# Two recurrent layers on one core: 32x32 inverses turned by VectorE, delta scores paired, single steps moved by one half slot

## What is computed

```
dq, dk_, dv_ = split(causal_conv_silu(dn_qkv)); dq, dk_ = l2norm(dq), l2norm(dk_)
# per head: with the decay between tokens and beta, strictly lower A = beta * (k k^T) * decay
# T = (I + A)^-1 ; u = T (beta v) ; o = (q k^T * decay) u
h_b = rmsnorm(o, dn_norm_w) * silu(dn_z)
```

```
h_a = rmsnorm(mlstm(q, k, v, i, f)) * ml_norm_w * sigmoid(ml_o) * silu(ml_z)
y = sigmoid(gate_a) * (h_a @ w_out[:2048]) + sigmoid(gate_b) * (h_b @ w_out[2048:])
```

## Time and profile before

| what | value |
|---|---|
| median of 3 runs | 2379.36 us (2378.09 to 2380.82) |
| profiled execution, own time | 2380.18 us |
| its span, first to last instruction | 2378.4 us |
| PE busy | 2362.0 us (99%) |
| DVE busy, ACT busy, POOL busy | 1426.4, 1183.9, 241.7 us |

### The profile page before, as it was taken

How to read it: one execution, slowest core, us unless ns; L and a number is a source line. 1 busy time by engine, 2 the same in 40 slices (tenths; PEclk the granted TensorE clock), 3 DMA queues, 4 the chain that set the end, 5 groups by cost and what they waited for, 6 DMA issues and landing times.

```text
span 2378.4 us, 28485 instructions
## 1 busy us (share of the span) xinstructions
PE 2362.0 (99%) x11452; PEld 1939.2 (82%) x11452; DVE 1426.4 (60%) x1701; ACT 1183.9 (50%) x1695; POOL 241.7 (10%) x336
## 2 busy tenths in 40 slices
PE   9999999999999999999999999999999999999998
PEld 7887888888888888888887778788888888888887
DVE  6655665665566545665865565576554554557775
ACT  6544454454445444555655455465444444446554
POOL 0053004305300430000000010000000000000000
PEclk9999999999999999999999999999999999999999
DMA  6565457446545655666665454456555555655554
GB/s 211 195 173 164 142 178 190 157 154 183 167 137 182 174 169 169 222 206 194 211 216 190 142 179 149 152 179 227 186 188 195 189 184 194 193 181 193 195 194 142
DMA packets 241073, 430.79 MB, mean 181 GB/s; under 512 B 32212, under 2 KB 35933, under 8 KB 240942
## 3 DMA queue, kind: packets, MB, share of 16 engines
q1 hardware_dynamic: 227808, 413.38, 54.4%
q10 hardware_dynamic: 13134, 15.60, 2.2%
HBM read 423.66 MB, written 5.29 MB: 180 GB/s over the span
## 4 chain that ended last, share of the span: by engine, by line
PE 89%; POOL 5%; DVE 2%; DMA 1%; issue 1%; ACT 1%; ACTq 0%; SPq 0%; POOLq 0%; DVEq 0%
PE gemm L1328 27%; PE gemm L1330 27%; PE gemm L1329 27%; POOL arena L2283 5%; PE side L904 3%; DMA arena<-delta_blocks 1%; DVE arena L1751 1%; DVE weight_lo L1745 1%; PE side L1251 1%; PE side L998 0%; PE side L1266 0%; PE side L1290 0%; DMA arena<-in_x_dram 0%; PE side L1064 0%; PE side L1220 0%
## 5 line engine op out<-in xcount | busy, mean ns | idle before, releaser
L1745 DVE TENSOR_TENSOR weight_lo<-weight_raw,weight_hi 128x1024 fp32r<-128x1024 f32 x780 | 970.5, 1248 | 736.3 <-ACT weight_hi L1356 735.0
L1356 ACT ACTIVATE weight_hi<-weight_raw 128x1024 fp32r<-128x1024 f32 x780 | 821.9, 1056 | 863.2 <-PE gemm L1330 822.7
L1328 PE MATMUL gemm<-weight_hi,x_hi 128*128 128x512 f32 x2368 | 943.8, 399 | 1.1 <-DVE weight_lo L1745 1.1
L1330 PE MATMUL gemm<-weight_hi,x_lo 128*128 128x512 f32 x2368 | 924.6, 390 | 0.0
L1329 PE MATMUL gemm<-weight_lo,x_hi 128*128 128x512 f32 x2368 | 924.0, 390 | 0.0
L1328 PEld LDWEIGHTS gemm<-weight_hi,x_hi 128*128 128x128 f32 x2368 | 445.4, 188 | 100.2 <-issue 9.7
L1330 PEld LDWEIGHTS gemm<-weight_hi,x_lo 128*128 128x128 f32 x2368 | 445.2, 188 | 94.3
L1329 PEld LDWEIGHTS gemm<-weight_lo,x_hi 128*128 128x128 f32 x2368 | 445.9, 188 | 88.9 <-issue 1.4
L1328 PE MATMUL gemm<-weight_hi,lhs_hi 128*128 128x512 f32 x736 | 287.4, 390 | 0.0
L1330 PE MATMUL gemm<-weight_hi,lhs_lo 128*128 128x512 f32 x736 | 286.8, 390 | 0.0
L1329 PE MATMUL gemm<-weight_lo,lhs_hi 128*128 128x512 f32 x736 | 286.7, 390 | 0.0
(11 more groups left out here) (186 smaller groups left out, 1024.0 us busy)
## 6 DMA issues: line engine op xcount, KB each, us to landing
weight_raw<-in_w_in_dram SPq DMA_DIRECT2D x207, 1024.0 KB, 5.1
weight_raw<-in_w_out_dram SPq DMA_DIRECT2D x48, 1024.0 KB, 5.1
weight_raw<-in_w_gate_dram SPq DMA_DIRECT2D x44, 1024.0 KB, 5.2
weight_raw<-in_w_up_dram SPq DMA_DIRECT2D x44, 1024.0 KB, 5.1
weight_raw<-in_w_down_dram SPq DMA_DIRECT2D x44, 1024.0 KB, 5.0
arena<-rel_line ACTq DMA_DIRECT2D x8, 384.0 KB, 5.3
arena<-delta_blocks ACTq DMA_DIRECT2D x16, 128.0 KB, 5.2
arena<-in_x_dram ACTq DMA_DIRECT2D x4, 512.0 KB, 6.0
```

The lines of the kernel that those rows point to most:

```text
L1328: e.matmul(pair[i][:, :], xh[:, s], wh, start=first, stop=False)
L1330: m = e.matmul(pair[i][:, :], xl[:, s], wh, start=False, stop=last)
L1356: return e.activation(o, i, ACT.Copy, scale=scale)
L1745: return e.tensor_tensor(o, x, y, op)
```

## The change

1. `dT` moves from PE and ACT to DVE: one `transpose` instruction on the whole tile of 128x1024 (eight 128x128 matrices), which turns each 32x32 block in place of its own. It waits for `tin`. The two PSUM banks of `dT` and its two ACT copies are gone.
2. The tile `N` of `dinv` now counts as live until `tout` has landed, so its block is given out later, and the homes of many later tiles differ.
3. The six `dsc` steps stand two a half slot: s+8 to s+10 in place of s+8 to s+13.
4. `dnorm` (all four groups, q and k), the chain `mnum`, `msq`, `mgated`, `mout` of pr = 1 and 3, and `gout` of the second pair of GLA heads stand one half slot later.

```
-            put(END[key] + 7, "dnorm", key, 0), put(END[key] + 7, "dnorm", key, 1)
+            put(END[key] + 8, "dnorm", key, 0), put(END[key] + 8, "dnorm", key, 1)
...
-            put(s + 8 + z, "dsc", g, q)
+            put(s + 8 + z // 2, "dsc", g, q)
...
-        put(s + 31, "dT", g, 0), put(s + 31, "dT", g, 1)
+        put(s + 31, "dT", g)
...
-        s = END[f"mz{pr}"] + 2 if pr % 2 else END[f"dz{pr}"] + 45
+        s = END[f"mz{pr}"] + 3 if pr % 2 else END[f"dz{pr}"] + 45
...
-    put(t + 1 + hp, "ggated", hp), put(t + 2 + hp, "gout", hp, 0), put(t + 2 + hp, "gout", hp, 2)
+    put(t + 1 + hp, "ggated", hp), put(t + 2 + 2 * hp, "gout", hp, 0), put(t + 2 + 2 * hp, "gout", hp, 2)
...
-        live(("N", g), ("nin", g), ("pool:dinv", g))
+        live(("N", g), ("nin", g), ("dma:tout", g))
...
-        live(("U", g), ("dT", g, 0), ("pe:du1", g))
+        live(("U", g), ("dT", g), ("pe:du1", g))
...
-        def dT(g, i):
-            w.wait_ge(*at("dma:tin", g))
-            p, Tt = open_bank("dT", g, i), heads(blk("Tt", g), i)
-            for h in range(HB):
-                m = turn(p[:, h * P:(h + 1) * P], Tt[:, h, :])
-            m.then_inc(sem("pe:dT"))
...
-        def dT(g, i):
-            U = claim("U", g)
-            w.wait_ge(*at("pe:dT", g, i))
-            copy(part(U, i), bank("dT", g, i)).then_inc(sem("act:dT"))
...
+        def dT(g):
+            U = claim("U", g)
+            w.wait_ge(*at("dma:tin", g))
+            e.transpose(U, blk("Tt", g)).then_inc(sem("dve:dT"))
```

More of the change, by code:

```diff
@@ L398 @@
 for _engine, _names in {
-        "pe": "cols0 cols xturn gate1 fsum rel1 convturn dnorm dsc dT dX dv du0 dbu du1 do dout chan mdec mscore "
+        "pe": "cols0 cols xturn gate1 fsum rel1 convturn dnorm dsc dX dv du0 dbu du1 do dout chan mdec mscore "
               "mturn mnum mout ggate2 gsum gscore gkend gstate go gout alog aturn apv fturn",
-        "act": "xturn sqsum kept tanh convtap convsilu dnorm dT du0 du1 donorm dout chan mexp mturn msq mout "
+        "act": "xturn sqsum kept tanh convtap convsilu dnorm du0 du1 donorm dout chan mexp mturn msq mout "
                "ggabs ggexp ggln gkend gsq gout aexp aturn apv fturn",
-        "dve": "cols xturn kept silu gate0 gate2 fsum rel0 rel1 convtap convsilu ddecay dsc dX dv dbu do "
+        "dve": "cols xturn kept silu gate0 gate2 fsum rel0 rel1 convtap convsilu ddecay dsc dT dX dv dbu do "
                "dgate mdec mm mden mgate mgated yb yhalf ya yres x1w gload ggate0 ggate2 ggate3 gscore ggated anorm res2 res4 fact "
@@ L522, in bank_table @@
     same = {"cols0": "dve", "cols": "dve", "fsum": "dve", "rel1": "dve", "dnorm": "act", "dsc": "dve",
-            "dT": "act", "dX": "dve", "dv": "dve", "du0": "act", "dbu": "dve", "du1": "act", "do": "dve", "dout": "act",
+            "dX": "dve", "dv": "dve", "du0": "act", "dbu": "dve", "du1": "act", "do": "dve", "dout": "act",
             "chan": "act", "mdec": "dve", "mturn": "act", "mout": "act", "gscore": "dve",
@@ L1018, in dX @@
             if wd < P:
-                w.wait_ge(*at("act:dT", g, 1))
+                w.wait_ge(*at("dve:dT", g))
                 p = open_bank("dX", g, wd)
@@ L1336, in tensor_program @@
         steps = dict(cols0=cols0, cols=cols, xturn=xturn, gate1=gate1, fsum=fsum, rel1=rel1, convturn=convturn, dnorm=dnorm,
-                     ddecay=ddecay, dsc=dsc, dT=dT, dX=dX, dY=dY, dv=dv, du0=du0, dbu=dbu, du1=du1,
+                     ddecay=ddecay, dsc=dsc, dX=dX, dY=dY, dv=dv, du0=du0, dbu=dbu, du1=du1,
                      do=do, dout=dout, chan=chan, mdec=mdec, mscore=mscore, mturn=mturn, mnum=mnum, mout=mout,
@@ L1723, in scalar_program @@
         steps = dict(cols0=cols0, cols=cols, xturn=xturn, sqsum=sqsum, kept=kept, tanh=tanh, gate1=gate1, rel0=rel0,
-                     rel1=rel1, convtap=convtap, convsilu=convsilu, dnorm=dnorm, ddecay=ddecay, dT=dT,
+                     rel1=rel1, convtap=convtap, convsilu=convsilu, dnorm=dnorm, ddecay=ddecay,
                      nin=nin, tin=tin, du0=du0, du1=du1, donorm=donorm, dout=dout, chan=chan, mm=mm, mexp=mexp, mturn=mturn, msq=msq,
@@ L2263, in vector_program @@
                      gate2=gate2, fsum=fsum, rel0=rel0, rel1=rel1, convtap=convtap, convsilu=convsilu, dss=dss,
-                     ddecay=ddecay, dsc=dsc, dX=dX, dY=dY, dv=dv, dbu=dbu, do=do, donorm=donorm,
+                     ddecay=ddecay, dsc=dsc, dT=dT, dX=dX, dY=dY, dv=dv, dbu=dbu, do=do, donorm=donorm,
                      dgate=dgate, mdec=mdec, mm=mm, mscore=mscore, mden=mden, mgate=mgate, msq=msq, mgated=mgated,
```

## The result

The kernel after the change takes **2392.06 us** (median, 2391.87 to 2393.78) against 2378.90 us for the kernel before (2378.09 to 2380.82): ratio **1.0056**, 95% interval 1.0038 to 1.0073. The change makes the kernel slower by 13.2 us. The profiled execution took 2392.19 us with a span of 2390.3, so 12.0 us more than that of before (11.9 by the spans). The prediction was 2390.8.

The account below looks back on a forecast made before the run. PE was taken as the bound, busy 2362.0 of 2378.4 us. Terms -3.5 - 0.1 - 1.4 - 1.6 + 14.6 + 3.4 = +11.4 us on the median 2379.36 gave 2390.8 us; 8 in 10 for 2383 to 2395.

Parts of the forecast that it names:

- `dT` off PE: Four groups on PE: each visit of 8 transposes removed saves 0.88 us, 3.5 us in all.
- pairs of `dsc`, PE's own time: Score steps on PE: 12 visits fewer, with next to no fixed price each; 0.1 us gained, bounds 0 and 1.1.
- block `N`, waits of the stream: Third mdec of both mLSTM groups: DVE no longer waits for dinv, both product stream waits go, 0.92 + 0.49 = 1.4 us gained.
- `dnorm` dq2 and `gout`: Side steps on PE that waited for DVE by 0.94 and 0.69 us; one half slot later they gain 1.6 us.
- `dnorm` dk0: One of the other dnorm steps on PE, said to have waited for nothing and to gain nothing.
- waits at `mout`, new less old: PE before mout of pr = 1 and 3: new waits 7.6 and 8.6 us, old 1.6 gone, 14.6 us lost.
- lower clock behind them: PE's clock behind the two mout waits: 1.7 us lost for each, 3.4 in all; bounds 0 and twice that.
- The chain from `tin` to `mout`: From ACT's issue of tin, through msq, POOL's power and mgated, until PE starts mout: 8.3 us.
- The rival that the waits vanish: At mout: tout lands 5.8 and 6.8 us sooner than the rows have, all waits go, 2371.2 us; chance 0.11.
- milder cases: At mout: dinv doesn't slide (2387.2), the clock isn't lost (2387.4), or neither (2383.8); chance together 0.2.
- the slide of `dinv`: dinv, tout and tin come 2 x 0.91 = 1.8 us later against the half slots, as all six scores precede nin.
- all that follows is in the times of before: Chain of pr = 1 and 3: waits computed in the earlier trace's times, upstream gains left out as shifting PE and dinv alike.

Follow-up runs that it names:

- the chain alone: Kernel before with only the chain mnum, msq, mgated, mout of pr = 1 and 3 one half slot later: 2396.41 us, ratio 1.0072.
- single scores: Kernel after with the six dsc steps in six half slots again: 2387.89 us, ratio 1.0037.
- the chain back: Kernel after with the chain of pr = 1 and 3 at its old half slots (END + 2) again: 2379.10 us, ratio 0.9997.
- the needless matmuls: Kernel after with 38 matmuls of unused result on PE ahead of its wait in mout of pr = 1 and 3: 2388.69 us, ratio 1.0042.

## Why the prediction was right

The sum of the prediction against the trace of after, in us. Rows of the profiled executions are compared, whose own times differ by 12.0 and whose spans by 11.9. The third column holds how much later or sooner PE's product stream stands behind each place, so that it leaves only 0.1 us without one.

| term | predicted | in the trace | by a run of its own |
|---|---|---|---|
| `dT` off PE | -3.5 | -3.6 | -3.8 |
| pairs of `dsc`, PE's own time | -0.1 | -0.4 | see below |
| block `N`, waits of the stream | -1.4 | -1.7 | -1.3 |
| `dnorm` dq2 and `gout` | -1.6 | -1.8 | -2.2, with the next row |
| `dnorm` dk0 | nothing | -0.5 | |
| waits at `mout`, new less old | +14.6 | +17.1 | |
| lower clock behind them | +3.4 | +3.2 | +3.4 |
| start of the program | not foreseen | -0.5 | |
| sum | +11.4 | +11.8 | |

**Right, and shown.** The cause is the order of ACT's queue, told by the program order and nothing else: with `tin` behind `msq` the loss turns into a gain of 6.5 us (2373.04 against 2379.56). The chain from `tin` to `mout` was added up from rows at other times and, in part, of another pair to 8.3 us and is 8.26 in the kernel after, 8.26 with the chain alone and 8.25 with single scores (at pr = 3 8.26, 8.62 and 8.32). The clock term was measured apart at 3.4. The rival that the waits vanish (2371.2) named what decides, the landing of `tout` against the chain; in the trace of after `tin` would have had to be issued 8.97 us sooner. Neither of the milder cases came: `dinv` slid, and PE stood at the lower level behind both waits.

**In part luck.** The size of the clock term rested on one fall of the clock at the start of the program, which none of the other eleven traces shows. And the sum is as near as it is because two errors offset each other: the waits were put 2.5 us too low, the gains 1.9 us too low, of which 0.5 are a wait of `dnorm` that the prediction says isn't there ("The other `dnorm` steps waited for nothing"), 0.3 the pairs and 0.5 the start of the program.

**Mis-sized: the slide of `dinv`.** I put it at 1.8 us, two scores. PE reached `mout` at 449.97 - 8.97 = 441.00 and would have reached it in the kernel before, one half slot on, at 441.46 + 2.72 = 444.18, so PE runs 3.18 us ahead of its old times there; `dinv` ends at 437.78 as before at 437.76. The slide is therefore 3.2. The 1.8 are all in the issue of `nin`, at 392.40 after against 393.76: -1.36, and 3.18 less 1.36 is 1.8, as predicted. What I left out is behind it. POOL of after and of before:

```profile
392.40 1.92 ACTq L1492 DMA_DIRECT2D arena<-delta_blocks  x4
...
400.15 36.90 POOL L2276 TENSOR_TENSOR arena<-arena 128x1024 f32<-128x1024 f32 x63 [11.62 <-DMA arena<-delta_blocks]
```

```profile
400.41 36.64 POOL L2283 TENSOR_TENSOR arena<-arena 128x1024 f32<-128x1024 f32 x63 [3.27 <-DMA arena<-delta_blocks]
```

From the issue until POOL starts it is 7.75 us, against 400.41 - 393.76 = 6.65: 1.1 more, and `dinv` itself 0.3 more. The step of the prediction that failed is "all that follows is in the times of before": the transfer and `dinv` took another time once they stood at another place. At pr = 3 the wait is 9.75 for a predicted 8.6, with 8.14 us from the issue to POOL's start against 7.32. Why the transfer took longer no run shows.

**Weak: the price of the pairs.** "I take 0.1" is the price on PE, and the slide was charged to the chain alone. As a part by itself the pairs cost 9.1 us in the kernel before and 4.2 in the kernel after. The prediction took over the waits of the earlier trace rows without asking what ended them; it was POOL, by its power behind `dinv`, as the last two rows on POOL and DVE of the kernel with pairs alone show. Whoever had asked would have seen that the waits of the kernel before grow by every us that `dinv` slides. In the whole change this stayed hidden, for the gate at `tin` is later than the one on POOL.

**Why the parts don't add up.** Alone they measure -3.8, -1.3, -2.2, +9.1 and +16.9, together +18.7, but the change measures +13.2. The 9.1 of the pairs is where the difference lies: 4.9 of it is gone once the chain is late and `N` has its own time. By the traces 2.1 of that are the waits of the stream at `mdec`, which a late `dinv` no longer makes, and 2.0 are at `mout`, where the pairs cost 6.5 us alone and 4.5 in the kernel after: there the gate at `tin` is the later one anyway. The remaining 0.6 between the sum and the change can't be told from noise.

**Not foreseen, and small.** The fall of the clock at the start of the program, 1.6 us in the trace of before, is missing from that of after, as it is from all ten others; PE waited 1.1 us more at 21 us for the low part of x instead. Both belong to the single execution as far as the runs tell, for the change touches nothing there. By the medians the change costs 13.2, by the two traces 12.0: the profiled execution of before, 2380.18, lies 1.3 above its median, that of after 0.1 above its own.

## What to carry to other kernels

When a step moves by one place in a table, look up on every engine that takes part in it what it now stands behind, the DMA issues above all: an issue that waits for a landing holds the compute instructions behind it, and PE paid 8.97 us for a `msq` whose input was ready. Ask of every wait, the short ones too, which gate ended it and which is the next one: here a chain had one gate on ACT and one on POOL, and the first hid what the second had come to cost. And time such a change by parts: without the pairs, and with `tin` put behind `msq`, the rest of it gives 2370.28 against 2378.99, while the whole was slower.

## What the runs showed of the hardware

**The landing of a small load is not a constant.** The time from the issue of `nin` of g = 1 until POOL starts `dinv` was 7.63 to 7.89 us in the five kernels with paired scores (after, the chain back, `tin` behind, the needless matmuls, pairs alone) and 5.88 to 6.99 in the seven with single ones. For the other three groups the mean is longer with pairs too, by 0.4 to 0.8 us, but the ranges overlap (g = 2: 6.24 to 8.04 against 6.18 to 7.17). In the kernel with pairs alone, the two weight loads issued between 388 and 404 us took 7.0 us to land, against 5.5 in the kernel before; `nin` moves 0.5 MB beside the weights in both. That the two get in each other's way is likely, but no run kept them apart.

**A split on DVE holds up one instruction of POOL.** `dinv` of g = 0 took 33.4 to 33.5 us in the four kernels in which DVE waits for its end and the scores are single, and 35.2 to 35.9 in the seven in which `N` is kept and DVE goes on working. Before and after:

```profile
165.62 33.37 POOL L2283 TENSOR_TENSOR arena<-arena 128x1024 f32<-128x1024 f32 x63 [4.18 <-DMA arena<-delta_blocks]
```

```profile
166.97 35.24 POOL L2276 TENSOR_TENSOR arena<-arena 128x1024 f32<-128x1024 f32 x63 [11.50 <-DMA arena<-delta_blocks]
```

The same 63 small instructions, 1.9 us more; with the pairs alone, where DVE stands longest, it is 32.32. The single instructions say why. Windows of 1.1 us in the trace of before, the first under a split of DVE that runs from 171.84 to 173.07, the second without one (columns: PE, PEld, DVE, ACT, POOL, each with its count of instructions):

```profile
171.90:173.00 1.10, 1.10 (x7) 0.91 (x6) 1.10 (x1) 0.00 (x0) 1.10 (x1) 1.00 0.62 108
173.60:174.70 1.10, 1.10 (x12) 1.10 (x11) 0.00 (x0) 0.79 (x2) 0.86 (x4) 1.00 1.04 404
```

Beside the split POOL is at one instruction all the time, without it it touches four. It is so in all 48 `dinv` of the twelve traces, their first two instructions left out: 515 instructions took over 0.8 us, and every one of them ran beside a `weight_lo` split; none of the 1667 that met no work of DVE did. Not every one beside a split was slow: 365 were not. In g = 0 seven slow ones make 32.3 us, eight 33.4 to 33.5, ten 35.2 to 35.9; in g = 1 twelve make 35.8 to 36.6 and thirteen, which all six kernels with the late chain have, 36.9 to 37.6. The Trainium skill (SBUF — State Buffer, SBUF: two separate sides) says that VectorE and GpSimd share one pair of ports, which one of them holds for a whole instruction while the other is blocked, if the VectorE instruction has two inputs in SBUF or runs in a mode that uses both ports. The split has two inputs in SBUF, so the rows agree. The wait that `N` took from DVE was in part paid back in this way, since two more splits now run beside `dinv`, and `dinv` ends later for it.

**The transpose of 32x32 blocks.** 1.24 us for 128x1024 in float32, the same for all four. The Trainium skill (Vector Engine (DVE) Microarchitecture Reference, 3.8 The reshape front-end and per-opcode configuration) gives one element per cycle and lane, from which the prediction made its estimate of 1.07 us; the measurement is 0.17 above it, and close to what the plain two-input splits of the same shape take here (1.22).

**The clock behind a wait.** Waits of PE of 2.55 us (chain back) already brought the lower level with them (the transposes take 1.56 us there), those of 0.81 and 1.2 (`tin` behind `msq`) did not. At the start of the program an idle time of 2.02 us had the lower level behind it in the trace of before, and one of 2.36 us in the kernel with the needless matmuls had not (granted clock 1.00 from 11 to 15 us), so the length of the wait alone doesn't decide. Nor does it set the price: behind waits of 2.5 to 3.8 us the lower level cost 1.5 to 1.6, behind 6.6 and 7.9 us with the chain alone 2.0 and 2.6, behind 9.0 and 9.8 us 1.6 each.
